# Delta rule: gate running sums broadcast by DMA from DRAM scratch instead of by TensorE transposes, and an attention division moved by one slot

## The reference, cut to what matters

```python
g = jnp.cumsum(g..., axis=-1)                        # the gate's running sums
diff = g[..., :, None] - g[..., None, :]
decay = jnp.exp(jnp.where(causal, diff, -jnp.inf))
a_strict = jnp.where(strict, beta[..., :, None] * kk * decay, 0.0)
qk = jnp.einsum('bnhik,bnhjk->bnhij', q, k) * decay
...
s_own = jnp.where(rel_own[None] >= 0, s_own, NEG_INF)   # second block's attention
p = jax.nn.softmax(s_own, axis=-1)
return jnp.einsum('hqs,hsd->hqd', p, v_own)
```

## Time and profile before

| | |
|---|---|
| median of 3 runs | 2914.6 us (2909.82, 2914.6, 2914.79) |
| the profiled execution: its time, its span | 2910.18 us, 2908.4 us |
| PE, DVE, ACT, POOL busy | 98%, 74%, 51%, 16% of the span |
| mean granted TensorE clock | 0.998 |
| delta stage with its heads in the loops | 78 to 775 us of the span |
| second block's attention | 1920 to 2040 us of the span |

### The profile page before, as it was taken

One profiled execution on the slowest core, in us unless ns is written; L12 is line 12 of the kernel. 1 busy time (PEld: TensorE's weight loads), 2 busy tenths in 40 slices (PEclk: granted clock), 3 DMA queues, 4 the chain that ended last, 5 costly groups with the idle time before them and its releaser, 6 DMA issues.

```text
span 2908.4 us, 50758 instructions
## 1 busy us (share of the span) xinstructions
PE 2855.3 (98%) x17162; PEld 2496.8 (86%) x17162; DVE 2154.5 (74%) x3164; ACT 1489.3 (51%) x2140; POOL 452.3 (16%) x188
## 2 busy tenths in 40 slices
PE   7999999999999999999999999999999999999998
PEld 6888888888888888888897888888898888888887
DVE  6777777777588888888878888976786446565466
ACT  4455444444344444444445788865545444444443
POOL 0111101111000000000000000000004445455443
PEclk9999999999999999999999999999999999999999
DMA  6544444545568888788876545566785566667655
GB/s 238 168 152 150 156 160 157 164 163 171 167 218 303 304 305 317 288 302 312 308 268 206 174 167 174 175 207 227 261 304 174 192 209 242 238 226 249 204 182 180
DMA packets 199095, 637.03 MB, mean 219 GB/s; under 512 B 32312, under 2 KB 46776, under 8 KB 198208
## 3 DMA queue, kind: packets, MB, share of 16 engines
q1 hardware_dynamic: 165024, 601.92, 59.5%
q10 hardware_dynamic: 33952, 33.52, 3.6%
HBM read 619.61 MB, written 15.75 MB: 218 GB/s over the span
## 4 chain that ended last, share of the span: by engine, by line
PE 62%; issue 25%; DVE 6%; ACT 3%; DMA 2%; DVEq 0%; SPq 0%; ACTq 0%; POOL 0%; POOLq 0%
PE gemm L591 37%; PE gemm L595 19%; DVE wl L1635 2%; ACT wh L1057 1%; DMA raw<-in_stream 1%; PE gemm L588 1%; PE gemm L589 1%; DVE dT L1833 1%; DVE dW L1831 1%; DVE cc L1640 0%; DVE gB L1853 0%; ACT gA L1158 0%; DVE cb L1640 0%; ACT gB L1151 0%; PE side L726 0%
## 5 line engine op out<-in xcount | busy, mean ns | idle before, releaser
L591 PE MATMUL gemm<-xs,wh 128*128 128x512 f32 x5088 | 1608.4, 397 | 11.3 <-DVE cb L1640 3.4
L1057 ACT ACTIVATE wh<-raw 128x1024 fp32r<-128x1024 f32 x939 | 983.3, 1058 | 946.7 <-PE gemm L595 813.8
L1635 DVE TENSOR_TENSOR wl<-raw,wh 128x1024 fp32r<-128x1024 f32 x811 | 1033.1, 1279 | 427.2 <-ACT wh L1057 400.8
L595 PEld LDWEIGHTS gemm<-xs,wl 128*128 128x128 f32 x5088 | 955.3, 188 | 213.0
L595 PE MATMUL gemm<-xs,wl 128*128 128x256 f32 x5088 | 1004.9, 279 | 0.0
L591 PEld LDWEIGHTS gemm<-xs,wh 128*128 128x128 f32 x5088 | 772.7, 188 | 40.3 <-issue 23.3
L591 PE MATMUL gemm<-hid,wh 128*128 128x512 f32 x2112 | 664.3, 396 | 4.9 <-DVE xacc L1655 2.3
L595 PEld LDWEIGHTS gemm<-hid,wl 128*128 128x128 f32 x2368 | 436.0, 188 | 90.3
L595 PE MATMUL gemm<-hid,wl 128*128 128x256 f32 x2368 | 467.2, 279 | 0.0
L1563 POOL TENSOR_TENSOR wl<-raw,wh 128x1024 fp32r<-128x1024 f32 x128 | 348.0, 2724 | 362.5 <-ACT wh L1057 361.2
L591 PEld LDWEIGHTS gemm<-hid,wh 128*128 128x128 f32 x2112 | 318.4, 188 | 7.6 <-issue 2.9
(11 more groups left out here) (406 smaller groups left out, 1953.4 us busy)
## 6 DMA issues: line engine op xcount, KB each, us to landing
raw<-in_stream SPq DMA_DIRECT2D x940, 512.0 KB, 4.0
ada_a<-in_ada SPq DMA_DIRECT2D x144, 512.0 KB, 5.1
ada_b<-in_ada SPq DMA_DIRECT2D x48, 512.0 KB, 4.8
stash<-stage ACTq DMA_DIRECT2D x12, 512.0 KB, 2.9
att<-stash ACTq DMA_DIRECT2D x8, 384.0 KB, 4.3
x<-in_x SPq DMA_DIRECT2D x4, 512.0 KB, 5.7
A_scratch<-gB ACTq DMA_DIRECT2D x8, 256.0 KB, 3.6
Em<-E_scratch ACTq DMA_DIRECT2D x8, 256.0 KB, 6.4
```

Source lines behind the costliest of these rows:

```text
L591: mm(G[n][:, :], w, moving, start=first, stop=False, skip_group_check=True)
L595: op = mm(G[n][:, 0:T] if whole else G[n][:, T:2 * T], wl[:, slot, at:at + P], rhs(sl * SLAB_K + k)[:, 0:T], start=False, stop=last, skip_ ...
L1057: A(wh[:, slot, :], raw[:, slot, :], ACT.Copy).then_inc(hi_ready, 1)
L1635: tt(wl[:, slot, :], raw[:, slot, :], wh[:, slot, :].bitcast(F32), ALU.subtract).then_inc(lo_ready[slot], 1)
```

## The change

1. The four broadcasts of `gsel` per head on TensorE (L704) and the copy on GpSimd (L1575) go; `ps1` isn't written at step 1 any more.
2. Once, in the first head: TensorE transposes all running sums, `gcum`, 128x32 to 32x128 (slot 43), DVE copies them to `grow` (slot 44), ACT writes them to DRAM `gates_scratch` (slot 45), waits for it and issues the first broadcast read (slot 47).
3. Per head: a DMA on ACT's queue reads one row of `gates_scratch` (2 KB) into all 128 partitions of `gbc` (256 KB). It is issued at the end of ACT's step 1 for the next head, so a head's rows are asked for a whole head (about 85 us) before they are used.
4. DVE's `gB` and `gA` and ACT's `eg` read `gbc` in SBUF instead of `ps1` in PSUM; DVE waits for the row besides.
5. In the second block's attention the division of heads with odd h stands at k = 2 instead of k = 3, and one block of `x` moves from slot 17 to slot 28.

```diff
+    grow = nc.alloc_sbuf_tensor_at("grow", [32, P], F32, offset=hid_at + 14 * 2 * T * 4)
+    gbc = nc.alloc_sbuf_tensor_at("gbc", [P, 4, P], F32, offset=hid_at + 15 * 2 * T * 4)
+    gates_dram = nc.dram_tensor("gates_scratch", (QK_HEADS, 4 * P), F32).ap()
+    gates_moved = loads["x0"]
-    GATE_PE, GATE_ACT = {24: 0, 31: 1, 39: 2}, {12: 0, 35: 1, 37: 2, 41: 3}
-    GATE_DVE = {14: 0, 27: 1, 34: 2, 36: 3, 38: 4, 40: 5, 42: 6}
+    GATE_PE, GATE_ACT = {24: 0, 31: 1, 39: 2, 43: 3}, {12: 0, 35: 1, 37: 2, 41: 3, 45: 4, 47: 5}
+    GATE_DVE = {14: 0, 27: 1, 34: 2, 36: 3, 38: 4, 40: 5, 42: 6, 44: 7}
-    X_AT = (11, 11, 12, 13, 13, 15, 17, 19, 19, 20, 21, 21, 23, 33, 33, 35)
+    X_AT = (11, 11, 12, 13, 13, 15, 19, 19, 20, 21, 21, 23, 28, 33, 33, 35)
@@ PE, gates
+            elif step == 3:
+                pe.wait_ge(S("gate_dve"), 6)
+                nc.tensor.transpose(ps1[0:32, 0:P], gcum[:, :, :].rearrange("p h c -> p (h c)"), ident
+                                    ).then_inc(S("gate_pe"), 1)
@@ PE, delta, s == 1
                 for j in range(4):
-                    nc.tensor.transpose(ps0[:, j * P:(j + 1) * P], rn[:, j:j + 1].to_broadcast([P, P]), ident)
-                for j in range(4):
-                    op = nc.tensor.transpose(ps1[:, j * P:(j + 1) * P], gsel[:, j:j + 1].to_broadcast([P, P]), ident)
+                    op = nc.tensor.transpose(ps0[:, j * P:(j + 1) * P], rn[:, j:j + 1].to_broadcast([P, P]), ident)
                 op.then_inc(S("p_bc"), 1)
@@ ACT
+        def rows_of(it):
+            row = gates_dram[it:it + 1, :] if isinstance(it, int) else gates_dram[bass.ds(it, 1), :]
+            act.dma_start(gbc[:, :, :].rearrange("p a i -> p (a i)"), row.to_broadcast([P, 4 * P])).then_inc(gates_moved, 16)
...
+            elif step == 4:
+                act.wait_ge(S("gate_dve"), 7)
+                act.dma_start(gates_dram.rearrange("i (a p) -> (i a) p", p=P), grow[:, :]).then_inc(gates_moved, 16)
+            elif step == 5:
+                act.wait_ge(gates_moved, 32)
+                rows_of(0)
@@ ACT, delta, s == 1
-                A(eg[:, :, :], ps1[:, :].rearrange("p (v c i) -> p v c i", v=2, c=2)[:, :, 1, :],
+                A(eg[:, :, :], gbc[:, :, :].rearrange("p (v c) i -> p v c i", c=2)[:, :, 1, :],
                   ACT.Exp).then_inc(S("a_eg"), 1)
...
+                if not isinstance(it, int) or it + 1 < QK_HEADS:
+                    act.wait_ge(S("a_eg"), it + 1)
+                    rows_of(it + 1)
@@ POOL, s == 0
-                    nc.gpsimd.tensor_copy(gsel[:, :], gcum[:, bass.ds(2 * it, 2), :])
@@ DVE, gates
+            elif step == 7:
+                dve.wait_ge(S("gate_pe"), 4)
+                nc.vector.tensor_copy(grow[:, :], ps1[0:32, 0:P]).then_inc(S("gate_dve"), 1)
@@ DVE, delta, s == 1
                 dve.wait_ge(S("p_bc"), it + 1)
-                pv = ps1[:, :].rearrange("p (j i) -> p j i", j=4)
+                dve.wait_ge(gates_moved, 16 * it + 48)
+                pv = gbc[:, :, :]
                 tt(gB[:, :, :], pv, four(H("mask_s")), ALU.add).then_inc(S("d_gB"), 1)
@@ DVE, second block's attention
-            elif k == 3:
+            elif k == 3 - h % 2:
                 dve.wait_ge(S("ba_e"), B_HEADS + h + 1)
```

More of the change, by code:

```diff
@@ L197, in program @@
     qe = place("qe", [P, 2, P])
-    gsel = place("gsel", [P, 4])
     gcum = place("gcum", [P, V_HEADS, 2])
```

## The result

| | before | after |
|---|---|---|
| median | 2913.07 us (2909.82 to 2914.79, 4 runs) | 2935.31 us (2932.09 to 2936.7, 4 runs) |
| ratio | | 1.008, 95% interval 1.0068 to 1.0092 |
| span of the profiled execution | 2908.4 us | 2930.3 us |

The change makes the kernel 22 us (0.8%) slower; 2940 was forecast. Lines moved a little: L1844 and L1847 (gB, gA) are now L1865 and L1868, the split L1635 is L1652, GpSimd's three rotary instructions are L1600, L1601 and L1603, PE's step of the dilated attention at slot 9 is L813 and `vnat` is L1223.

What follows compares the result with a forecast made beforehand. DVE and ACT's chain from slot 2 to slot 16 was taken as the bound. 30.6 + 0.8 + 0.2 - 4.4 = +27.2 us on 2910.2 gave 2937.4, plus 2.2 towards the median: 2940, range 2918 to 2955.

Steps and rivals of the forecast that it cites:

- The bound: From slot 2 to slot 16 of each head, DVE and ACT's slackless chain to the bank bounds, not PE.
- The removed transposes gain nothing: Four PE transposes per head, 0.43 us, 3.4 us in all: PE only waits longer at the bank, gain nil.
- Both inputs in SBUF beside GpSimd: In each head gB and gA stand until GpSimd's rotary instructions end: gA 3.8 us later, 30.6 us in all.
- The hope that an SBUF input is quicker: DVE's SBUF inputs quicker than PSUM, about 0.06 us for each of 16 instructions, 1 us; nothing was taken.
- They take turns: The waiting engine precedes the other's next instruction: gB stands behind GpSimd's first rotary instruction, ending 2.2 us later, gA behind its second.
- the row of the last stage: Trace evidence for turns: DVE's L1991 starts while a GpSimd instruction has long been waiting, and takes 3.43 us, 8 times.
- the first rival: In each head gB keeps DVE's turn, only gA stands: +1.6 us per head, 12.8, giving 2922; chance 0.10.
- The one-stand rival: Same as the first rival: only gA stands, +1.6 us per head, 2922 us; chance 0.10.
- ACT's issue: One DMA issue per head between the last exponential and `wh`: 0 to 0.37 us, 0.1 taken, 0.8 us in all.
- the 4 us that the range held for `A_scratch` in the queue: The row's DMA might hold up `A_scratch` on ACT's queue: up to 0.5 us per head, kept for the range only.
- The division: Odd heads' division moved ahead in the attention: between 3.5 and 4.6 us of PE's waits gained, 4.4 taken.
- Where PE would show it: PE waits before its steps 2 and 3 and at the bank, 3 to 5 us per head in sum.

Runs made afterwards that it cites:

- e11: Changed kernel with GpSimd's rotary instructions held back until gA is made: 2922.24 us, ratio 1.0037.
- e6: Changed kernel with TensorE's four transposes of gsel back; gB and eg read PSUM, only gA reads SBUF: 2929.53 us, ratio 1.0064.
- e8: Changed kernel with gB, gA, eg and their exponentials made one head ahead, at slots 40 to 42: 2893.34 us, ratio 0.994 to the kernel before.
- e9: Changed kernel with GpSimd's three rotary instructions per head made tiny, rotation of q and k left out: 2907.42 us, ratio 0.9987.
- e10: Kernel before the change with GpSimd's three rotary instructions per head made tiny, rotation left out: 2910.84 us, ratio 1.0001.
- e3: Changed kernel with all its DMAs, issues and waits, but TensorE's four transposes back and gB, gA, eg reading PSUM: 2905.89 us, ratio 0.9982.
- e7: Changed kernel with the two qkv scalings, which read PSUM, moved ahead of gB on DVE: 2935.28 us, ratio 1.0083.
- e4: Changed kernel with gB, gA, eg and their exponentials made one head ahead at slot 44, next rows issued at slot 26: 2953.98 us, ratio 1.015.

## Why the prediction was right, and where it wasn't

- **The bound: right.** From slot 2 to slot 16 DVE and ACT hand each other the work without slack. e11 adds 2.03 us there and a head grows by 2.04, e6 adds 2.90 and it grows by 2.90 (each to 0.2 us); e8 takes work out and it shrinks.
- **The removed transposes gain nothing: right** as far as e9 against e10 can tell (a head 0.10 us apart, 0.43 would be the whole).
- **Both inputs in SBUF beside GpSimd: right**, shown from both sides by e3 and e9. The hope that an SBUF input is quicker was rightly left out (0.67 us in both).
- **They take turns: wrong for `gB`.** This is the step that failed. `gB` was said to stand 2.2 us in all heads and did in one; the row of the last stage was no fair likeness, since there the DVE instruction followed a split that had stood itself, as `gA` in e7 follows a `gB` that had. With `gB` through, the first rival's course came, `gA` 1.5 us late.
- **The split behind: missing.** The one-stand rival ended with `gA` and gave 2922. The step that it left out is the split of 103.71, which had been only 0.19 us ahead of GpSimd's third instruction. 1.5 us more put it behind: 1.9 us a head. 1.5 + 1.9 = 3.4 is near the forecast's 3.8, so the forecast of 2940 was close for a reason that was half another one: a stand of `gB` that didn't come and a stand of the split that nobody had counted happen to cost about the same. That part was luck.
- **ACT's issue: not seen.** 0.8 us were taken and e3 shows none, nor the 4 us that the range held for `A_scratch` in the queue. **The division: right**, 4.4 us taken, the 4.6 us of wait gone and 4.9 measured.
- **The sum.** 27.2 us were forecast, and the two profiled executions lie 2930.3 - 2908.4 = 21.9 us apart. Of the 5.3 between them 3.0 are the stands (3.8 taken, 3.43 found, 8 heads), 0.8 the issues and 0.5 the division; 1.0 is left, no more than single executions of one kernel differ by.
- **Where PE would show it: half right.** It waits 3.3 us a head as said, but at slot 9 for `vnat`, not before steps 2 and 3 (1.4 us before step 2 in head 1, where `gB` stood). The qe instruction is back at 0.41 us (L1881, median 409 ns) as said.

## What to carry to other kernels

Before an operand moves from PSUM to SBUF on DVE, look what GpSimd does in those microseconds, and then look at the next two-SBUF instruction too: a stand of 1 us can push it behind GpSimd's next instruction and cost 2 us more. If an engine waits at the end of a chain, take work out of that chain rather than off the waiting engine: four transposes less on PE gained nothing, the decay work moved ahead, a few slots away from a bank hand-over, gained 12 us (8 x 1.53), and placed right at the hand-over it lost 44 (7 x 6.25) and 4.8 more in head 0.

## What the runs showed of the hardware that was not expected

- DVE can run two two-SBUF instructions in a row past a waiting GpSimd (GpSimd's L1600 stood for 3.88 - 2.38 = 1.5 us, over the split and `gB`), but didn't once the first of them had stood itself (e7, 8 of 8). One head in eight, always head 1, went the other way for `gB` in three kernels.
- A stand of PE can cost about twice its length. After the 4 us of idleness in e4 the clock fell from 2.4 to 1.2 GHz, which took 3.4 us of full speed by the rows above. In the changed kernel it fell too (0.59 from 114 to 118 us, after the wait: 0.41 x 4 = 1.6 us), and a head still grew by no more than DVE's chain did, 3.49 against 3.43. A part of the slower matmuls fits in what the wait for the bank and the removed transposes had taken before (0.44 + 0.43 us in head 0); where the rest went isn't shown.

```profile
110.00:114.00 4.00, 0.70 (x5) 0.41 (x3) 1.23 (x4) 3.23 (x11) 0.00 (x0) 0.98 0.61 197
114.00:118.00 4.00, 3.79 (x15) 3.47 (x16) 3.75 (x10) 2.05 (x3) 0.00 (x0) 0.59 0.47 130
```
